# Loads moved into earlier stages of a decoder step, and a row sum in another order of row groups

## The reference

```
h   = x * (1 + scale1) + shift1              # six rows from silu(c) @ w_ada
P   = h @ w_in                               # q, k, v (4 heads x 2 x 64 | 4 x 2 x 64 | 4 x 128), B, C, u (512 each)
A   = softmax(q1 k1^T/8 + bias) - lambda * softmax(q2 k2^T/8 + bias);  oA = RMSNorm_head(A v)
oB  = B * dwconv3_causal(C * u)
x   = LayerNorm(alpha*x + gate1 * (concat(oA, oB) @ w_out))
x   = LayerNorm(alpha*x + gate2 * PEER(x * (1 + scale2) + shift2))   # 128 retrieved experts per token
```

## Time and profile before

| what | value |
|---|---|
| median of 3 runs | 3984.93 us (3982.57 to 3989.07) |
| profiled execution: own time | 3991.51 us |
| its span, first to last instruction | 3989.5 us |
| mean granted PE clock | 0.714 of full speed |
| DMA, mean over the span | 337 GB/s, 1343.89 MB |
| prompt attention | about 480 to 649 us of the span |
| sample attention | about 649 to 1020 us |
| mix | about 1020 to 1194 us |

### The profile page before, as it was taken

The page is one execution under the profiler, slowest core; times in us unless marked ns, Lnnn a source line. Parts: engine busy times, 40 slices in busy tenths (PEclk is TensorE's granted clock), DMA queues, the critical chain, the costliest instruction groups (busy, mean ns, idle before and its releaser), DMA issues. The chain is left out here.

```text
span 3989.5 us, 55293 instructions
## 1 busy us (share of the span) xinstructions
PE 2409.4 (60%) x16678; PEld 1084.2 (27%) x16678; DVE 2542.6 (64%) x6416; ACT 1465.6 (37%) x4223; POOL 1296.8 (33%) x1334
## 2 busy tenths in 40 slices
PE   5999776898765354553564465465356456446543
PEld 3446445565322121220121121122112112112110
DVE  1111165666475888677677677767757767767775
ACT  0110053333003455543434444444444344444443
POOL 0000001444002344443444344444344444444442
PEclk7999978999887565775675676566567567657655
DMA  9102134999328899999999999999999999999998
GB/s 359 49 33 61 24 1 144 407 411 387 138 92 315 353 396 404 421 420 421 411 417 413 419 415 418 403 421 412 421 407 418 419 406 420 421 420 414 419 412 333
DMA packets 245932, 1343.89 MB, mean 337 GB/s; under 512 B 47288, under 2 KB 60825, under 8 KB 94084
## 3 DMA queue, kind: packets, MB, share of 16 engines
q0 software_dynamic: 164352, 1174.49, 71.4%
q1 hardware_dynamic: 64072, 147.14, 10.9%
q10 hardware_dynamic: 17212, 18.74, 1.4%
HBM read 1319.30 MB, written 20.97 MB: 336 GB/s over the span
## 5 line engine op out<-in xcount | busy, mean ns | idle before, releaser
L1595 PE MATMUL psum<-sb_ring,sb_fold_weighted 128*32 128x256 f32 x8448 | 1008.9, 569 | 1307.6 <-PEq L62 1203.0
L1563 POOL DMA_INDIRECT sb_ring<-in_uv,sb_experts x1056 | 1151.4, 1090 | 1655.6 <-POOLq L62 1504.6
L1780 DVE CUSTOM_DVE_ANT_0 sb_ring<-sb_ring,sb_h_four 128x1024 f32<-128x1024 f32 x1056 | 1265.8, 1225 | 652.6 <-DMA sb_ring<-in_uv,sb_experts 615.4
L1595 PEld LDWEIGHTS psum<-sb_ring,sb_fold_weighted 128*32 128x32 f32 x8448 | 268.6, 134 | 2012.8 <-issue 2003.2
L1685 ACT ACTIVATE sb_gelu<-sb_dots 128x1 f32<-128x1 f32 x1056 | 210.3, 199 | 994.4 <-ACTq L62 985.8
L806 POOL DMA_DIRECT2D sb_v_pages<-in_cache_v x256 | 135.0, 527 | 861.5 <-issue 683.5
L1690 ACT ACTIVATE sb_fold_weighted<-sb_fold,sb_expert_w 128x32 f32<-128x32 f32 x1056 | 339.3, 321 | 34.4
L1618 PE MATMUL psum<-sb_w_pq,sb_h2T 128*128 128x512 f32 x576 | 336.6, 738 | 1.5 <-issue 1.5
L1687 ACT ACTIVATE sb_expert_w<-sb_gelu,sb_gates 128x1 f32<-128x1 f32 x1056 | 311.1, 295 | 34.5
L1664 ACT COPY sb_h_four<-sb_h_tiles 32x1024 f32<-32x1024 f32 x180 | 187.5, 1042 | 4.2
L1618 PEld LDWEIGHTS psum<-sb_w_pq,sb_h2T 128*128 128x128 f32 x576 | 132.4, 242 | 193.4 <-issue 193.4
(11 more groups left out here) (227 smaller groups left out, 2646.7 us busy)
## 6 DMA issues: line engine op xcount, KB each, us to landing
sb_k_pages<-in_cache_k SPq DMA_DIRECT2D x256, 256.0 KB, 6.1
sb_v_pages<-in_cache_v POOLq DMA_DIRECT2D x256, 256.0 KB, 6.2
sb_w_ada<-in_w_ada SPq DMA_DIRECT2D x12, 2048.0 KB, 17.0
sb_ring<-in_uv,sb_experts POOLq DMA_INDIRECT x1056
sb_w_qkv<-in_w_in SPq DMA_DIRECT2D x3, 2048.0 KB, 19.3
sb_w_bcu<-in_w_in SPq DMA_DIRECT2D x12, 512.0 KB, 6.3
sb_w_pq<-in_w_pq SPq DMA_DIRECT2D x3, 2048.0 KB, 17.1
sb_h_tiles<-h_scratch SPq DMA_DIRECT2D x9, 512.0 KB, 9.2
```

The source lines that it names most:

```text
L1563: pool.indirect_dma_start(ring[:, slot, :], None, uv, bass.IndirectOffsetOnAxis(ap=experts[:, u, g, n:n + 1], axis=0))\
L1595: ins = nc.tensor.matmul(psum[q * NS:(q + 1) * NS, bank, at:at + QUARTER], fw[:, slot, :], ring[:, slot, D + q * QUARTER:D + (q + 1) * QUA ...
L1780: dot = nc.vector.tensor_tensor_reduce(ring[:, slot, 0:D], ring[:, slot, 0:D], h2x[:, half], 1.0, 0.0, ALU.mult, ALU.add, dots[:, slot:slo ...
```

## The change

Five edits.

1. The strip of the bias is loaded in conv, by SP behind the last weights, into a buffer that `project` hands on; prompt attention neither loads it nor waits for it.
2. The page table, and the keys and values of chunks 0, 1 and 2, are loaded in prompt attention: 12 key loads on SP ahead of the 18 small stores, 12 value loads on POOL, which did nothing there. The stage waits for them at its end. Sample attention begins its loads at chunk 3, and PE does not wait for the first three chunks. The four small loads of `row_consts` now stand ahead of the page loads of SP.
3. `q_rows` is cleared and filled by DVE at the start of prompt attention.
4. `w_out` is loaded by SP at the end of sample attention, when the values of chunk 63 have landed; SP waits for it there. Its buffer lies where the strip and qT were. mix no longer loads it or waits for it.
5. The 32 matmuls of the sum run over the samples outside and the heads inside, so that neighbours use different row groups of the array and different banks.

```diff
+def load_pages(eng, pt, cache, slots, k, land):
+    u = k % DEEP
+    pages = [eng.value_load(pt[0:1, k * CH + g:k * CH + g + 1], min_val=0, max_val=POOL - 1) for g in range(CH)]
+    for g, page in enumerate(pages):
+        eng.dma_start(slots[g::CH, u, :, :].rearrange("q j n -> q (j n)"),
+                      cache[ds(page, 1)].rearrange("a (q j) n -> (a q) (j n)", j=CH))\
+            .then_inc(land, 16)
...
@@ conv, SP
+                for h in range(H):
+                    f = toep_dram[h].rearrange("q m -> (q m)")[P - 1:P - 1 + P * (TOEP - 1)]
+                    sp.dma_start(strip[:, h, :], f.rearrange("(q m) -> q m", q=P)[:, 0:STRIP]).then_inc(strip_land, 16)
+                sp.wait_ge(strip_land, 16 * H)
@@ prompt_attention, SP, POOL, DVE
-                for h in range(H):
-                    f = toep_dram[h].rearrange("q m -> (q m)")[P - 1:P - 1 + P * (TOEP - 1)]
-                    sp.dma_start(strip[:, h, :], f.rearrange("(q m) -> q m", q=P)[:, 0:STRIP]).then_inc(strip_land, 16)
+                sp.dma_start(pt[:], A["page_table"].rearrange("(a b) n -> a (b n)", a=1)).then_inc(tab, 16)
+                sp.wait_ge(tab, 16)
+                for k in range(DEEP):
+                    load_pages(sp, pt, A["cache_k"][0].rearrange("g p h m d -> g p (h m d)"), kp, k, k_land)
...
+                sp.wait_ge(k_land, 16 * CH * DEEP)
+            @block.gpsimd
+            def _(pool):
+                pool.wait_ge(tab, 16)
+                for k in range(DEEP):
+                    load_pages(pool, pt, A["cache_v"][0].rearrange("g p h d -> g p (h d)"), vp, k, v_land)
+                pool.wait_ge(v_land, 16 * CH * DEEP)
...
-                dve.wait_ge(strip_land, 16 * H)
+                step(nc.vector.memset(q_all[:], 0.0))
+                step.done()
+                for h in range(H):
+                    for m in range(2):
+                        part = slice(m * DH, (m + 1) * DH)
+                        step(nc.vector.tensor_copy(q_all[part, :, h, m * NT:(m + 1) * NT],
+                                                   qT[part, h, SEQ:SEQ + NS].rearrange("p (b t) -> p b t", t=NT)))
+                step.reset()
@@ sample_attention
-                for k in range(STEPS):
+                sp.wait_ge(T["rows_zero"], 1)
+                for h in range(H):
+                    sp.dma_start(rows[head(h, M), :], A["const_rows"][h * M:(h + 1) * M, :]).then_inc(T["small"], 16)
+                for k in range(DEEP, STEPS):
                     load(sp, cache_k, kp, k_land, k_free, k)
+                last = STEPS - 1
+                sp.wait_ge(v_land[last % DEEP], last // DEEP * 16 * CH)
+                sp.dma_start(w_out[:], A["w_out"][0].rearrange("(k p) n -> p k n", p=P)).then_inc(T["w_land"], 16)
+                sp.wait_ge(T["w_land"], 16)
...
-                for h in range(H):
-                    for b in range(NB):
+                for b in range(NB):
+                    for h in range(H):
                         ins = nc.tensor.matmul(psum[0:NS, KT + h, 0:DV], combs[head(h), b, :], o_all[head(h), b, :],
@@ mix
-                sp.dma_start(w[:], A["w_out"][0].rearrange("(k p) n -> p k n", p=P)).then_inc(T["w_land"], 16)
...
-                pe.wait_ge(T["w_land"], 16)
```

More of the change, by code:

```diff
@@ L56 @@
 RING = 8
+CH = 4
+DEEP = 3
 def take(eng, sem, n=1):
@@ L141, in build @@
             with ExitStack() as att:
-                tensors |= dict(qT=sbuf(att, "qT", [P, H, SEQ + NS]), kT=sbuf(att, "kT", [P, H, SEQ + NS]),
-                                v=sbuf(att, "v", [P, TILES + 1, AW]))
-                project(**tensors)
+                tensors |= dict(kT=sbuf(att, "kT", [P, H, SEQ + NS]), v=sbuf(att, "v", [P, TILES + 1, AW]))
+                tensors["strip"] = project(**tensors)
                 end_stage()
+                tensors |= dict(q_all=sbuf(att, "q_rows", [P, NB, H, NS]), pt=sbuf(att, "page_table", [1, NB * PAGES], I32),
+                                kp=sbuf(att, "k_pages", [P, DEEP, CH, AW]), vp=sbuf(att, "v_pages", [P, DEEP, CH, AW]))
                 prompt_attention(**tensors)
                 end_stage()
+                until_att.close()
+                tensors["w_out"] = sbuf(until_mix, "w_out", [P, KD, D], side="right")
                 sample_attention(**tensors)
@@ L151, in build @@
             end_stage()
+            until_mix.close()
         peer(**tensors)
@@ L485, in project, with conv @@
         pre.close()
-        conv(nc, A, sem, sbuf, psum, hT, o_convT, zlast, zslast)
-def conv(nc, A, sem, sbuf, psum, hT, o_convT, zlast, zslast):
+        strip = sbuf(until_att, "bias_strip", [P, H, STRIP], side="right")
+        conv(nc, A, sem, sbuf, psum, hT, o_convT, zlast, zslast, toep_dram, strip)
+        return strip
+def conv(nc, A, sem, sbuf, psum, hT, o_convT, zlast, zslast, toep_dram, strip):
     with ExitStack() as st:
@@ L798, in load @@
         def load(eng, cache, slots, land, free, k):
-            u = k % DEEP
-            pages = [eng.value_load(pt[0:1, k * CH + g:k * CH + g + 1], min_val=0, max_val=POOL - 1) for g in range(CH)]
-            if k >= DEEP:
-                eng.wait_ge(free[u], k // DEEP)
-            for g, page in enumerate(pages):
-                eng.dma_start(slots[g::CH, u, :, :].rearrange("q j n -> q (j n)"),
-                              cache[ds(page, 1)].rearrange("a (q j) n -> (a q) (j n)", j=CH))\
-                    .then_inc(land[u], 16)
+            eng.wait_ge(free[k % DEEP], k // DEEP)
+            load_pages(eng, pt, cache, slots, k, land[k % DEEP])
         with nc.Block() as block:
@@ L987, in _ @@
                 step = Steps(dve, dve_c)
-                step(nc.vector.memset(q_all[:], 0.0))
                 step(nc.vector.memset(rows[:], 0.0))
                 step.tell(T["rows_zero"])
-                for h in range(H):
-                    for m in range(2):
-                        part = slice(m * DH, (m + 1) * DH)
-                        step(nc.vector.tensor_copy(q_all[part, :, h, m * NT:(m + 1) * NT],
-                                                   qT[part, h, SEQ:SEQ + NS].rearrange("p (b t) -> p b t", t=NT)))
-                step.tell(T["q_ready"])
                 step(nc.vector.memset(rel[BUCKETS:BUCKETS + 1, :], MASKED))
```

48 lines of the change are left out of this document (18 added, 30 removed).

## The result

The changed kernel took **3949.74 us** (median of 4 runs, 3948.36 to 3952.99), the kernel before, timed beside it, 3983.75 us (4 runs, 3981.36 to 3989.07). The forecast was 3941.8 us with a range of 3933 to 3955. The direction and the range held. The gain was forecast as 43.1 us, so the size needs explaining. Two of the causes were not in the forecast at all: where the profiled execution of before had lost its time, and the place at which the page numbers are read.

A forecast was written before the change was run, and what follows sets the result against it. Transfers were taken to bound peer and sample attention, leaving gains at stage ends and between. Terms 15.4 + 16.4 + 5.3 + 6.0 = 43.1 us off 3991.51 gave 3948.4, less 6.6 for the median 3941.8 us; range 3933 to 3955.

The forecast's parts named there:

- baseline step: Whole kernel: 3948.4 us from the profiled execution, less 6.6 us because the median lies that far below it, gives 3941.8.
- the strip's term: Start of prompt attention: DVE's first bias at 483.55 instead of 499.02, a gain of 15.4 us.
- the rival that something else than the strip held DVE: Prompt attention: DVE's code or the small stores kept it until 499; total gain 27.7, median 3957.2 us; chance 0.06.
- cost nothing: Prompt attention: 24 page transfers, 15.5 us, end near 500 with over 100 us of cover; only the stage's end awaits the stores.
- Forecast 16.4: Start of sample attention: first scores at 657.4 instead of 673.73, a gain of 16.4 us.
- Afterwards nothing differs: Sample attention after its first scores: slots equally filled in both kernels, so 5.07 us a step stays for 63 steps.
- the head start is given back: Sample attention: loads set the end, so the start brings 10 instead of 16.4 us; 3948.2 us; chance 0.07.
- the two chains: End of sample attention: the sum, copied at 1012.1, against w_out, waited for until 1014.3; w_out sets the end, gain 5.3 us.
- Mix: Start of mix: PE's wait for w_out goes and the broadcast rows land earlier, so the product ends 6.0 us earlier.
- the slack that was called 5.5 us: Mix: the rows land at about 1037.8 and DVE is ready at 1042.8, ahead of the product at 1048.3.
- that smallest sum: Low end of the likely gain: 13.8 + 14 + 4.1 + 4.5 give 36.4 us, before 3 us for scatter.
- The slow rival: Sample attention: PE stays at the low clock, 3.5 us a step, 224 us over 64 steps, time 4166 us; chance 0.03.

The follow-up runs named there:

- second execution of before: The kernel before, unchanged, profiled once more: 3984.95 us (span 3982.9).

## Why the prediction was right, and where its size was off

**The baseline step failed.** "The median of the runs lies 6.6 us below that execution, so the median should be 3941.8 us." That takes the 6.6 us off as if they stood in a stretch that no edit touches. The second execution of before shows that 3.7 of them stood in the strip's wait, the very wait that the change removes, 0.9 in mix's start, which it shortens, and 2.0 in the attention behind the strip, which is 147.7 us in the changed kernel's profiled execution and 146.8 there. Taking that second execution for a typical one (3984.95 us, where the medians of before are 3983.75 and 3986.51), the strip's term is 14.9 − 3.2 = 11.7 us, not 15.4. The forecast counted the long wait as gain and then took it off once more. Without that step it would have read 3948.4, 1.3 us from the median, though by terms that miss in both directions (below), so that nearness would be luck too.

**The strip: right in place, its length not explained.** "That one is the wait" (the 16.7 us transfer) was right about what DVE waited for, and the first bias came where it was forecast. Why one transfer took 16.7 us was not asked, and the forecast took the whole wait for the strip's own. The strip needs 9.1 to 9.3 us from the barrier when large loads or nothing follow it, and 14.9 to 18.5 when the small stores follow. The forecast named the small stores only in the rival that something else than the strip held DVE.

**Pages in prompt attention: "cost nothing" held, and hid a gain.** Of the stores the forecast said that only the end of the stage waits for them. In the changed kernel that was so. But with the first chunks out of their way the same stores came first and lengthened the biases by 11.8 us. Standing behind 12 loads they cost under 1 us.

**Sample attention: mis-sized by 3.7 us.** Forecast 16.4, measured 12.7. "Afterwards nothing differs" was the wrong step. The helper also moved the reads of the page numbers behind the wait for the slot, 2.2 us at POOL's first restart, and undoing that alone gives 3.5 us: 336.6 us for the stretch, which is 352.8 − 16.2. The diff showed the move plainly, and the trace of before showed the load 0.7 us behind the product without it. The forecast's size then holds, its mechanism only in part. It let the earlier first scores carry to the end one for one. They came 16.0 us earlier. But with the page numbers read early in both kernels, loading the chunks ahead of the stage moved the first scores by 13.6 to 15.3 us and the last values by 18.0, and starts made earlier inside the stage hardly arrived. The amount that left the stage, 6.3 MB, is 15.5 us at the 407 GB/s of the earlier trace rows, and that is what the runs bear out; that the shift of the first scores comes to nearly the same is luck. The clock was a smaller miss. The turn of chunk 0 was fast, that of chunk 1 slow, where the forecast had 3.68 and 3.37; other executions of the same stage had both fast.

**The rival "the head start is given back" was half right.** It was priced as a change of the start; it is true at the margin. 4.7 us more of head start brought 0.6 in one kernel, and 3.0 to 4.7 brought 1.5 in another; from 655 to 960 us the DMA engines are at a share of 1.01. But what the loads moved into prompt attention gave, 18 us, was kept: the stretch is 354.6 us with the chunks loaded in the stage and 336.6 with them loaded ahead, page numbers read early in both.

**The end of the stage: right.** Forecast a sum of 3.8 us, measured 3.64. Forecast w_out as the later of the two chains, with SP's wait over 13.8 us behind its issue; from the issue to mix's first issue it is 13.8, and the barrier's 1.1 is in that (1019.62, where ACT's copy ends, to 1020.71 before), so it landed after about 12.7. That is the 1.0 us by which the gain is larger than forecast. The estimate from the Trainium skill, "DMA: Bandwidth & Descriptors", section "Anatomy of one DMA", was 11.6 us; that section gives its fit for transfers on the gpsimd path, and w_out goes out on SP's queue. The trace lies midway between that and the forecast. The two chains nearly tie, and ACT's copy ends at 984.07.

**Mix: 7.6 us instead of 6.0.** The product came 6.0 us sooner for w_out, as forecast. The rest is subln, which now lands with nothing of size behind it. DVE scaled tile 0 at 992.04, 6.6 us behind SP's first issue, against 8.2 before (1028.86 and 1020.71); with w_out loaded in mix again it is 7.7. In the second execution of before it was 7.6 too, and the term 6.7 instead of 7.6. The rows were forecast 17.1 us behind SP's first issue and came at 19.4, so the slack that was called 5.5 us is 1.6, DVE's idle time ahead of L1359.

**The total.** Against the second execution of before the stretches give 11.7 − 0.9 + 13.0 + 6.3 + 6.7 = 36.8 us, less 0.8 by which the barrier of prompt attention came later: 36.0. The medians give 34.0, within the scatter of either kernel's runs. The range held, but its upper end does not follow from its terms: 3984.93 − 36.4 + 3 is 3951.5, not 3955. The measured 3949.74 lies below either. And the 14 and 4.5 us in that smallest sum were given without a working; the first of them measured 12.7 to 13.0. The slow rival did not come: from the third turn of keys on PE had the full clock, as the 1.06 or 1.07 us of the scores groups from 646.67 on show.

## What to carry to other kernels

Before subtracting the distance between a profiled execution and the median, find the stretch in which it lies: a second execution of the unchanged kernel shows it, and if the stretch is one that the change removes, nothing is to be subtracted. When a loop is refactored into a helper, read the order of every register read and wait on its queue, and not only the transfers: here the order of two lines took back a fifth of the gain at that place. In a stage at full DMA share, as this one, transfers moved out of the stage counted in full, while a start made earlier inside it mostly did not.

## What the runs showed of the hardware that was not expected

18 stores of 512 pieces of 4 bytes, 37 KB in all, lengthened prompt attention by 11.8 us (144.4 against 132.6 from the first bias to the last) where they were the first thing issued there, in three pauses of the engines, though no compute engine waits for them. They also stretched the wait for four loads issued ahead of them on the same queue from 9.3 to 14.9 us and more. Issued 16 us later in the same stage they cost nothing that could be seen. While they ran the DMA engines showed a share of about 1 to 2 at some 1 GB/s. The Trainium skill, "DMA: Bandwidth & Descriptors", section "Specifications", puts the least transfer for line rate at 512 bytes and says that smaller ones are done by read-modify-write. The trace agrees on the rate: a share of 1.89 at 1 GB/s, where pages of 256 KB move 407 GB/s at 1.01.

Four row groups of the array, 32 rows each, with a bank each, worked side by side: 64 records at the low clock (granted clock 0.50 in both) took 3.64 us in alternating order and 11.32 us in the other, a factor of 3.1.
